# A fused two-block transformer kernel: the forget-gate and rotary-key projections as fp32 products of 32 columns, four side by side, and block 2's entry reordered

## What is computed

```python
# block 1
h = rmsnorm(x); proj = h @ w_in[l]
q_a, f_a, i_a, g_a, u_b, g_b, q_c, k_c, v_c, g_c, f_c = split(proj)   # f_c: 8 columns
o_a = gated linear recurrence(q_a, f_a, i_a); o_b = window means(u_b)
log_f_c = log_sigmoid(f_c + fox_f_bias[l])      # per head; its cumulated sum biases the scores
o_c = causal softmax attention of 8 heads (q_c, k_c, v_c, log_f_c)
x = x + rmsnorm(concat(o_a, o_b, o_c gated) @ w_out[l])
# block 2
h = rmsnorm(x); proj = h @ w_in[l]
g_a, g_b, qa, ka, va, cq, ckv, kr = split(proj)   # kr: 32 columns, ka and va: 2 heads of 64
out_a = windowed attention with sinks (qa: 8 heads, ka, va: 2 heads shared by four each)
q = rmsnorm(cq) @ w_q_b;  k, v = rmsnorm(ckv) @ w_kv_b;  k_rope = rope(kr, positions)
out_b = causal attention of 8 heads on (q_nope, rope(q_rope)), (k_nope, k_rope), v
merged = sigmoid(g_a) * (out_a @ w_o_a) + sigmoid(g_b) * (out_b @ w_o_b)
x = x + rmsnorm(merged @ w_out);  x = x + rmsnorm(relu(rmsnorm(x) @ w_up)**2 @ w_down)
```

## Time and profile before

| | |
|---|---|
| Median of the runs | 987.54 us (986.87 to 987.56) |
| Profiled execution, its own time | 987.7 us |
| Its span, first to last instruction | 986.4 us |
| TensorE busy | 965.2 us (98%) |
| VectorE, ScalarE, GpSimd busy | 593.9, 425.4, 98.1 us |
| Chain that ended last | 82% TensorE, 12% VectorE, 3% ScalarE |
| TensorE's granted clock, mean | 0.993 of 2.4 GHz |

### The profile page before, as it was taken

How to read it: one execution, slowest core, us unless ns; L and a number is a source line. 1 busy time by engine, 2 the same in 40 slices (tenths; PEclk the granted TensorE clock), 3 DMA queues, 4 the chain that set the end, 5 groups by cost and what they waited for, 6 DMA issues and landing times.

```text
span 986.4 us, 13911 instructions
## 1 busy us (share of the span) xinstructions
PE 965.2 (98%) x5344; PEld 788.4 (80%) x5344; DVE 593.9 (60%) x1111; ACT 425.4 (43%) x816; POOL 98.1 (10%) x103
## 2 busy tenths in 40 slices
PE   9999999999999998999999999999999999999996
PEld 8878777767899765777777889988888888888895
DVE  7458778687758775766655742964154334434457
ACT  6355265355645253645544324563243224223421
POOL 2005105220210000000000313000000000000020
PEclk9999999999999998999999999999999999999998
DMA  6222111112325111211212352253323223322102
GB/s 250 84 88 64 65 43 65 44 64 76 107 86 190 57 54 31 72 52 56 82 44 69 103 192 69 90 227 106 107 86 95 99 86 107 104 88 90 39 1 86
DMA packets 25809, 86.74 MB, mean 88 GB/s; under 512 B 2960, under 2 KB 5712, under 8 KB 25488
## 3 DMA queue, kind: packets, MB, share of 16 engines
q1 hardware_dynamic: 23952, 80.25, 24.2%
q10 hardware_dynamic: 1552, 5.28, 1.5%
q0 software_dynamic: 240, 0.33, 0.1%
HBM read 81.65 MB, written 4.19 MB: 87 GB/s over the span
## 4 chain that ended last, share of the span: by engine, by line
PE 82%; DVE 12%; ACT 3%; issue 2%; DVEq 0%; ACTq 0%
PE PB L339 12%; PE PB L341 12%; PE PB L340 12%; PE PB L909 5%; PE PB L907 5%; PE PB L908 5%; PE PB L545 3%; PE PB L572 3%; PE PB L556 2%; DVE wl L1370 2%; DVE X L1426 2%; DVE AR L1423 2%; PE PB L370 2%; PE PB L789 1%; PE PB L790 1%
## 5 line engine op out<-in xcount | busy, mean ns | idle before, releaser
L339 PE MATMUL PB<-hh,wh 128*128 128x512 f32 x592 | 243.4, 411 | 0.0
L341 PE MATMUL PB<-hh,wl 128*128 128x512 f32 x592 | 232.1, 392 | 0.0
L340 PE MATMUL PB<-hl,wh 128*128 128x512 f32 x592 | 231.6, 391 | 0.0
L1370 DVE TENSOR_TENSOR wl<-raw,wh 128x1024 fp32r<-128x1024 f32 (+2 forms) x92 | 117.4, 1277 | 51.9 <-ACT wh L939 51.8
L339 PEld LDWEIGHTS PB<-hh,wh 128*128 128x128 f32 x592 | 111.8, 189 | 27.6 <-issue 5.6
L341 PEld LDWEIGHTS PB<-hh,wl 128*128 128x128 f32 x592 | 111.6, 188 | 24.4
L340 PEld LDWEIGHTS PB<-hl,wh 128*128 128x128 f32 x592 | 112.0, 189 | 23.7 <-issue 2.7
L939 ACT ACTIVATE wh<-raw 128x1024 fp32r<-128x1024 f32 (+2 forms) x92 | 93.3, 1018 | 52.1 <-PE PB L375 14.0
L1099 ACT ACTIVATE S<-S,sm 128x256 f32<-128x256 f32 (+3 forms) x96 | 50.8, 530 | 124.3 <-DVE sm L1462 86.5
L1370 DVE TENSOR_TENSOR wl<-AR,wh 128x1024 fp32r<-128x1024 f32 x55 | 67.6, 1230 | 43.3 <-ACT wh L939 43.3
L939 ACT ACTIVATE wh<-AR 128x1024 fp32r<-128x1024 f32 x55 | 57.8, 1052 | 70.3 <-PE PB L909 70.3
(11 more groups left out here) (353 smaller groups left out, 1735.2 us busy)
## 6 DMA issues: line engine op xcount, KB each, us to landing
AR<-in_dne SPq DMA_DIRECT2D x32, 512.0 KB, 3.6
AR<-in_upe SPq DMA_DIRECT2D x24, 512.0 KB, 3.5
raw<-in_w2g SPq DMA_DIRECT2D x16, 512.0 KB, 3.5
raw<-in_w1e SPq DMA_DIRECT2D x10, 512.0 KB, 3.5
raw<-in_w1q SPq DMA_DIRECT2D x8, 512.0 KB, 3.4
raw<-in_woab SPq DMA_DIRECT2D x8, 512.0 KB, 3.6
raw<-in_w2e SPq DMA_DIRECT2D x6, 512.0 KB, 3.9
X<-in_xT SPq DMA_DIRECT2D x4, 512.0 KB, 6.6
```

The source lines that it names most:

```text
L339: e.matmul(bank[:], a[:, col(k)], xa[:, k, :], start=k == 0, stop=False)
L340: e.matmul(bank[:], a[:, col(k)], xb[:, k, :], start=False, stop=False)
L341: i = e.matmul(bank[:], b[:, col(k)], xa[:, k, :], start=False, stop=k == 7)
L1370: e.tensor_tensor(low_, raw_of(c), high.bitcast(F32), ALU.subtract).then_inc(*up("lo", c))
```

## The change

1. `w1f` and a new chunk `w2r` (the 32 columns of `kr`, once) are weight tiles of 1024 by 32. They aren't split: VectorE multiplies the raw chunk by the input norm's gain into a tile `WN` (128 by 256), and `narrow` makes eight fp32 products of 32 columns with `X` itself, source tile `k` into rows `32 * (k % 4)` on of one bank. So four of them write the four quarters, and the four after them add to these. ScalarE has no `hi` for these chunks.
2. The four quarters of the bank are partial sums. For the gates ScalarE copies the last quarter (rows 96 to 103), and VectorE adds the other three one after the other, before the factor and the bias. For `kr` they are added by the permutation product: a new matrix `krm` sums the quarters and rotates, and the rotated key is formed on 32 rows instead of 128.
3. In block 1 `sums(0)` stands before the last `w1v` chunk and `spread(0)` ahead of `w1q` 0; ScalarE makes the root before `hi(6)`.
4. In block 2 the bank that `kr` had in `four_by_halves` takes the first query tile, so that five `w2e` tiles are left. The heads are paired 0 and 4, 1 and 5, 2 and 6, 3 and 7, so that each pair has one head of either key head: the keys need one copy, and the queries one operation with a scale per row (a column of `con`). `sums(1)` stands ahead of `w2e` 1 and `sums(3)` ahead of `w2e` 3.
5. The rotation of `kr` moves from ahead of the beats into them: its product to beat 6, in bank 6, its VectorE operations to beat 7. `lo` of `w2g` 9 moves behind the first `maxima`.

The diff, cut:

```diff
-    s = [("w1v", i, NW) for i in range(4)] + [("w1f", 0, NW), ("w1q", 0, NW), ("w1q", 1, NW)]
+    s = [("w1v", i, NW) for i in range(4)] + [("w1f", 0, 256), ("w1q", 0, NW), ("w1q", 1, NW)]
...
-    s += [("w2k", i, NW) for i in range(4)] + [("w2e", i, NW) for i in range(6)]
+    s += [("w2k", i, NW) for i in range(4)] + [("w2r", 0, 256)] + [("w2e", i, NW) for i in range(5)]
...
+            def narrow(c, bank, before):
+                e.wait_ge(*to("lo", c))
+                if before:
+                    e.wait_ge(*to(*before))
+                for k in range(8):
+                    i = e.matmul(bank[quarter(k)], WN[:, 32 * k:32 * k + 32], X[:, k, :], start=k < 4, stop=k > 3)
+                i.then_inc(*up("gemm", c))
...
-            c = CH["w1f", 0]
-            bank, _ = tenant(4, "fz")
-            e.wait_ge(*to("lo", c))
-            half(c, 0, bank, hh, hl)
-            e.wait_ge(*to("xs", 0, 7))
-            sums(0, 5)
-            half(c, 4, bank, hh, hl)
-            c = CH["w1q", 0]
-            bank, _ = tenant(7, "qk", 0, 0)
-            e.wait_ge(*to("lo", c))
-            half(c, 0, bank, hh, hl)
+                if n == 2:
+                    e.wait_ge(*to("xs", 0, 7))
+                    sums(0, 5)
+            narrow(CH["w1f", 0], *tenant(4, "fz"))
             spread(0, 6)
-            half(c, 4, bank, hh, hl)
+            tile(CH["w1q", 0], *tenant(7, "qk", 0, 0), hh, hl)
...
-            four_by_halves("w2k", (7, 2, 3, 0), [("cq", 0), ("cq", 1), ("cq", 2), ("kr",)], 1)
-            tile(CH["w2e", 0], *tenant(1, "qa", 0), hh, hl)
-            c = CH["w2e", 1]
-            bank, before = tenant(4, "qa", 1)
-            e.wait_ge(*to("lo", c))
-            e.wait_ge(*to(*before))
-            half(c, 0, bank, hh, hl)
+            four_by_halves("w2k", (7, 2, 3, 0), [("cq", 0), ("cq", 1), ("cq", 2), ("qa", 0)], 1)
+            narrow(CH["w2r", 0], *tenant(1, "kr"))
+            tile(CH["w2e", 0], *tenant(4, "qa", 1), hh, hl)
             e.wait_ge(*to("xs", 1, 7))
             sums(1, 5)
-            half(c, 4, bank, hh, hl)
-            c = CH["w2e", 2]
+            c = CH["w2e", 1]
...
+                if t == 6:
+                    e.wait_ge(*to("kr"))
+                    rotate(KR, 6, "rk", by=krm)
...
+            root(0)
             hi(6)
-            root(0)
...
+            e.wait_ge(*to("gemm", CH["w1f", 0]))
+            e.activation(z8, seat["fz",][96:104, :], ACT.Copy).then_inc(*up("fc"))
...
+                if PLAN[c][0] in NARROW:
+                    e.wait_ge(*landed(c))
+                    if PLAN[c][0] == "w2r":
+                        e.wait_ge(*to("gemm", CH["w1f", 0]))
+                    e.tensor_tensor(WN[:].rearrange("p (k n) -> p k n", k=8), raw_of(c).rearrange("p (k n) -> p k n", k=8),
+                                    pcol(NARROW[PLAN[c][0]], 8).unsqueeze(2).to_broadcast([128, 8, 32]),
+                                    ALU.mult).then_inc(*up("lo", c))
+                    return
...
-            e.tensor_tensor(z8, seat["fz",][0:8, :], R[0:8, :], ALU.mult).then_inc(*up("fz"))
+            e.wait_ge(*to("fc"))
+            for r in (64, 32, 0):
+                if r < 64:
+                    e.wait_ge(*to("fz", r + 32))
+                e.tensor_tensor(z8, seat["fz",][r:r + 8, :], z8, ALU.add).then_inc(*up(*(("fz", r) if r else ("fz",))))
             e.wait_ge(*to("fz"))
+            e.tensor_tensor(z8, z8, R[0:8, :], ALU.mult).then_inc(*up("fb", 0))
+            e.wait_ge(*to("fb", 0))
             e.tensor_scalar(z8, z8, par[0:8, P_FB:P_FB + 1], None, ALU.add).then_inc(*up("fb"))
...
+            e.wait_ge(*to("gemm", CH["w2r", 0]))
             e.tensor_tensor(KR, seat["kr",][:], R[:], ALU.mult).then_inc(*up("kr"))
             def queries(p):
-                e.wait_ge(*to("gemm", CH["w2e", p]))
-                for b in range(2):
-                    r = rows(b)
-                    e.scalar_tensor_tensor(QA[r, p, :], seat["qa", p][r, :], 0.125 * float(2.0 ** (2 * p + b + 1)),
-                                           R[r, :], ALU.mult, ALU.mult).then_inc(*up(*(("qa", p) if b else ("qa", p, 0))))
+                e.wait_ge(*to("gemm", CH["w2e", p - 1] if p else CH["w2k", 3]))
+                e.scalar_tensor_tensor(QA[:, p, :], seat["qa", p][:], con[:, C_QS + p:C_QS + p + 1], R[:],
+                                       ALU.mult, ALU.mult).then_inc(*up("qa", p))
...
             queries(0)
             queries(1)
-            lo(CH["w2e", 5])
+            queries(2)
+            lo(CH["w2e", 4])
             root(3)
-            queries(2)
-            lo(CH["w2g", 8])
             queries(3)
             row(3)
...
-            e.wait_ge(*to("gemm", CH["w2e", 4]))
-            bank = seat["ka",]
-            for g in range(2):
-                for b in range(2):
-                    e.tensor_tensor(KA[rows(b), g, :], bank[rows(g), :], R[rows(g), :], ALU.mult).then_inc(
-                        *up(*(("ka",) if g == b == 1 else ("ka", g, b))))
+            lo(CH["w2g", 8])
+            e.wait_ge(*to("gemm", CH["w2e", 3]))
+            e.tensor_tensor(KA, seat["ka",][:], R[:], ALU.mult).then_inc(*up("ka"))
...
-            lo(CH["w2g", 9])
-            e.wait_ge(*to("sn"))
-            rotated(KR, KR, 1.0, S[1], "rk")
-            e.wait_ge(*to("ro", "rk"))
             for t in range(BEATS2):
                 n, beat = divmod(t, 4)
                 if beat == 0 and n < 2 * STEPS:
                     maxima(2, n)
+                if t == 0:
+                    lo(CH["w2g", 9])
+                if t == 7:
+                    e.wait_ge(*to("rot", "rk"))
+                    e.wait_ge(*to("sn"))
+                    bank, r = seat["rks",], slice(64, 96)
+                    e.tensor_tensor(tmp[3][r, :], bank[0:32, :], SN[0:32, :], ALU.mult).then_inc(*up("rx", "rk", 0))
+                    e.tensor_tensor(KR[r, :], bank[r, :], CS[r, :], ALU.mult).then_inc(*up("rks"))
+                    e.wait_ge(*to("rx", "rk", 0))
+                    e.wait_ge(*to("rks"))
+                    e.tensor_tensor(KR[r, :], KR[r, :], tmp[3][r, :], ALU.add).then_inc(*up("ro", "rk"))
```

More of the change, by code:

```diff
@@ L298, in step, with head @@
             return p, i, lo, 128 * (i + 1 - lo)
+        def head(a, n, b):
+            p = step(a, n)[0]
+            return p + 4 * b if a == 2 and n < STEPS else 2 * p + b
         def scalars(n, b):
@@ L532, in scores @@
                     query = [QA[rows(b), p, col(i)] for b in range(2)]
-                    key = [KA[rows(b), p // 2, 128 * lo:128 * i + 128] for b in range(2)]
+                    key = [KA[rows(b), 128 * lo:128 * i + 128] for b in range(2)]
                 else:
@@ L743, in pe @@
             half(c, 4, bank, hh, hl)
-            c = CH["w2e", 3]
-            bank, before = tenant(5, "qa", 3)
-            e.wait_ge(*to("lo", c))
-            e.wait_ge(*to(*before))
-            half(c, 0, bank, hh, hl)
+            tile(CH["w2e", 2], *tenant(5, "qa", 3), hh, hl)
             e.wait_ge(*to("ca"))
             sums(3, 7)
-            half(c, 4, bank, hh, hl)
-            c = CH["w2e", 4]
+            c = CH["w2e", 3]
             bank, before = tenant(2, "ka")
@@ L1773, in dve @@
                 if k == 3:
[L1774 removed]
+                    lo(CH["w2e", 1])
+            lo(CH["w2e", 2])
+            root(1)
             lo(CH["w2e", 3])
[L1776 to L1777 removed]
             row(1)
```

67 lines of the change are left out of this document (40 added, 27 removed), and 1 row of the table SIGNALS.

## The result

The kernel after took 979.64 us (median of 4, 979.36 to 980.48); the kernel before 987.55 in the same set. The ratio is 0.9923, 95% interval 0.9906 to 0.9940: faster by 7.9 us or 0.8%, where 980.2 us was predicted.

A forecast was written before the change was run, and what follows sets the result against it. TensorE was taken as the bound, busy 965.2 of 986.4 us. Terms -6.9 - 0.3 - 0.8 + 0.7 = -7.3 us took 987.5 to 980.2 us; range 976.8 to 984.6.

The forecast's parts named there:

- Two tiles for two groups: Gate tile and one `w2e` tile, 5.44 us each, give way to eight narrow products of 1.97 us each group: -6.9 us.
- Rival A: Narrow products of different column groups don't run together: 7.1 us a group, kernel slower at 990.4 us; chance 0.06.
- Rival B: Passes of narrow products overlap by one only, a product's two being program neighbours: 4.1 us a group, 984.4 us; chance 0.11.
- Start of block 1: `w1e` 0 starts at 43.25 with its `lo` done at 42.85: no wait, 0 taken, up to 1 us if ScalarE is later.
- Entry wait: Entry of block 2: TensorE's 0.30 us wait for VectorE at 305.98 goes, -0.3 us (0 to -0.4).
- First turn: First beats of block 2: the first `turn`'s 0.76 us wait goes, -0.8 us (0 to -0.8).
- New wait: Second `turn` of block 2 waits for VectorE to read the rotated key from its bank: +0.7 us (0 to +1.6).
- rival C: The dip to 1.2 GHz from 378.0 to 384.6 goes: -3.0 us, so 977.2 us; chance 0.14.

The follow-up runs named there:

- the order test: Kernel after with the eight narrow products taking the column groups as 0,0,1,1,2,2,3,3 (gates) and 0,1,0,1,2,3,2,3 (rotated key): 980.32 us, before 986.36.
- the version with fewer column groups: Kernel after with the gates' narrow products in two column groups and the rotated key's in one, computing other sums: 986.48 us, before 986.59.
- the two versions without a dip in their traces: Kernel after with rotated queries' products in banks 5 and 2: 976.38 us; also rotated key's in 5 and first query half turned one beat sooner: 974.14.
- all three banks changed: Kernel after with the rotated key's product in bank 5 and the rotated queries' two products in banks 5 and 2: 975.69 us, before 986.59.

## Why the prediction was right, step by step

- **Two tiles for two groups: right.** Predicted 1.97 us a group, measured 1.95 in the first; the first maxima of block 1 start 3.44 us sooner (49.57 against 53.01), 3.47 predicted. That the law is "rounds of 0.85, as many as the fullest column group has products" was an inference from two groups; four, two and one group bear it out (a round is 0.86, going in and out 0.1 to 0.2). Rival A's price was right too (6.98 for 7.1), its mechanism false. Rival B's mechanism, neighbours in the program holding each other up, is excluded by the four records that start together, and by the order test. The estimate by the 2.38 times of the Trainium skill ("TensorE: Matmul & The Clock Gate", Part 3), 2.2 us a group, was too high: 1.95.
- **Start of block 1: right.** `w1e` 0 at 43.28 (43.25 predicted), its `lo` done at 42.97 (42.85), no wait.
- **Entry wait: right in kind, small in size.** 0.46 instead of 0.30, since I took the bracket and not the starts. The stretch from the narrow products to the first scores is 34.76 us (34.8 predicted).
- **First turn: right.** Its wait went; the maxima start 1.3 us behind the scores (1.5 predicted).
- **New wait: the step that failed.** I put +0.7 at the second turn, for VectorE's reading of the rotated key. That one isn't there. TensorE waited ahead of the product itself, for ScalarE's copy out of bank 6, and lost 1.25 us (0.8 once the next wait for ScalarE, hidden by it, is counted). I had asked who holds the bank after the product and not who holds it before: `tenant` names the copy, and ScalarE's queue has exponentials and a `hi` ahead of it. Because TensorE came later, VectorE was in time at the second turn (done at 351.87, the turn at 352.43): 1.25 earlier, the turn would have met my wait of 0.7, by these times; no run tested that.
- **The sum.** Terms as measured: -3.44 - 3.5 - 0.46 - 0.8 + 1.25 = -6.95. At equal clocks the two kernels differ by 6.8 to 7.0. The forecast was -7.3, and that the measured median came within 0.6 us of 980.2 is in part luck: the terms gave 0.35 less than forecast, and the clock 1.0 more.
- **The clock (rival C): half true.** I argued that the dip comes every time, from three runs of before within 0.7 us. That was the step too far: 17 runs show three groups, and its length changes without any change of the program. The first comparison had before mostly in the long group (987.5) and after in the middle one (979.4 to 979.8), which makes 7.9 of 6.9. The price of the whole dip was sized well: 3.0 predicted, 2.6 between the outer groups of before (987.39 less 984.75) and 2.9 by the traces (TensorE falls back that much in the dip of after against the version with fewer column groups, whose trace has the same waits and no dip).

## What to carry to other kernels

A weight of few columns should be spread over all column groups of 32; its time is that of one product times the number of products of the fullest group, and of the three orders tried none was dearer. When a product is moved into a queue, look up who must empty its bank before it and what stands ahead of that on its engine; a bank that has long been free took that wait away. A wait taken away is worth only what the next one leaves of it: follow the two traces on until their distance stays the same. If times fall into groups a fixed step apart, look at the granted clock by stretches, and compare group with group before you explain a microsecond.

## What the hardware showed that I had not expected

- Products for a free column group don't wait behind one whose group is busy: order 0,0,1,1,2,2,3,3 takes 1.87 us, as 0,1,2,3,0,1,2,3 does (1.86).
- Near TensorE's waits of 1.6 and 1.2 us (or one of 2.83 or 2.91) the clock fell to 1.2 GHz for 6.83 or 3.41 us or not at all, in executions of one program: 6.83 where it fell before the last of these waits was over (six traces), 3.41 where it fell 0.6 to 1.1 us after them (four traces, one of them behind a single wait of 1.64; another trace has a single wait of 1.63 and no dip). Of the two versions without a dip in their traces, the four runs each lie within 0.1 and 0.5 us. The Trainium skill ("TensorE: Matmul & The Clock Gate", "What's actually happening") ties the clock to how busy TensorE has been of late, and these traces agree; no run here shows what sets the moment at which it falls.
- A dip of 3.41 us cost 1.6 us in the kernel after, and nothing with all three banks changed, where the waits of 0.76 and 0.59 us behind it went in its place.
- At the start, the clock rose to 2.4 GHz between 3.9 and 5.8 us in twelve traces, and the first chunk began at 6.6 to 6.7; in two it rose at 7.1 and 7.2, and the chunk began at 7.05.
- A wait marked 0.30 or 1.09 us cost 0.46 and 1.25 from start to start, and the second of them 0.8 in the end.
